# Series of products that nobody reads, taken out of TensorE's program at every seam between stages

## The chip, the cores and the metric

One core of one Trainium2 chip. The metric is device time in microseconds (us); the kernel before took 1933.99 us, the median of 3 runs from 1933.72 to 1934.06.

## What is computed

Two models run one after the other on 256 tokens of width 1024, in float32, each with two layers.

- **First block** (twice): `h = rmsnorm(x) @ w_in`; three groups of attention heads on slices of h; `x += heads @ w_o`; then a feed-forward, `x += (silu(g) * u) @ w_down` with `g, u` the halves of a short causal convolution over `rmsnorm(x) @ w_up` (2 x 2816 columns). One more rmsnorm ends it.
- **Second block** (twice): a mixer (retention and HGRN2 heads on `rmsnorm(h) @ w_in`, 4608 columns, then `@ w_out`), and a mixture of 16 experts. `softmax(xn @ w_router)` gives each expert its 32 best tokens (top-k), and `ye = (silu(xe @ w_gate) * (xe @ w_up)) @ w_down`, times the gate, is added back to the tokens. A last rmsnorm gives the output.

## The kernel before

Every engine has one program, written out by hand; semaphores order them. The residual X stays in SBUF as two tiles of 128 tokens. Weights stream in through one hardware queue that SP issues, into a ring (6 slots in the first block, 12 and an arena beside them in the second); SP waits on `slot_free[s]`, which TensorE counts up behind the last product that reads a slot.

Between two stages stands a norm. ScalarE takes sums of squares (line 717, into XN), VectorE adds them (728), GpSimd takes the power -1/2 (736), VectorE and ScalarE scale one tile of 128 tokens each into XN (732 and 724). `turn_normed` (740) waits for these and transposes XN, four transposes to each of four PSUM banks (all at line 749); VectorE and ScalarE copy the banks to XT, and the next stage's products read XT: lines 2346 to 2348 (`up` of the feed-forward), 2099 to 2101 (first block's input), 2066 (the mixer's first block of columns). In the first block and in the mixer weights and activations are each split in two rounded parts, and every product is three.

Routing (2546 to 2558): logits (2520), softmax on VectorE and ScalarE, two transposes of the affinities (2549), four rounds of top-8 on VectorE (1971, 1973), two transposes of the slots (2554), one-hot rows (1987), and then, for each of four groups of four experts, `gather` (2579), products with quarters of the array (2621, 2639) for gate, up and down, and `scatter` (2671). In group 0 each block of weights is a separate piece (2621); later ones come in pairs (2639), and the very last block (the last `single_quad` of group 3) comes in two halves, waited for one after the other. `turn_gates` (2564) transposes the gates.

TensorE's queue is in order, so what stands in its program is carried out there. `idle_products(bank, n)` (2056) is n products of the identity with itself, 128x128, into a PSUM bank whose content nobody reads before it is written again. It stands at these places, with no wait ahead of it:

| where | n | line | times |
|---|---|---|---|
| before `turn_normed` of the feed-forward | 12 | 2332 | 2 |
| before `turn_normed` of the first block's second layer | 20 | 2072 | 1 |
| before `turn_normed` of the first mixer | 40 | 2388 | 1 |
| before `turn_normed` of the second mixer | 12 | 2388 | 1 |
| before the wait for the softmax | 5 | 2546 | 2 |
| before the wait for the top tokens | 20 | 2551 | 2 |
| before the wait for the one-hot rows | 6 | 2557 | 2 |
| before the last block of the last group | 7 | 2657 | 2 |

```python
def idle_products(bank, n):

    for _ in range(n):
        nc.tensor.matmul(psum[:, bank, 0:P], ident, ident, start=True, stop=True)
...
idle_products(4, IDLE_PRODUCTS["feed-forward"])
turn_normed(pe, past, 2, 1)
```

Of the kernel before, what the change touches and what calls it, by code (L numbers as in the profile page):

```python
# [15 lines left out]
P = 128  # L16
# [58 lines left out]
N_GROUPS = EXPERTS // GROUP  # L75
# [7 lines left out]
PAIRS = D // 256  # L83
# [19 lines left out]
ITEM_AT = {item: n for n, item in enumerate(ITEMS)}  # L103
EXP_LN_SET = "natural_log_exp_and_others"

IDLE_PRODUCTS = {"first block": 20, "feed-forward": 12, "first mixer": 40, "expert sums": 12,
                 "softmax": 5, "top tokens": 20, "one-hot rows": 6, "last quad": 7}
C2_N1, C2_N2, C2_LB, C2_OML, C2_FLAG, NPAR2 = 0, 8, 16, 20, 24, 28


# [32 lines left out]
def four_rows(k):  # L143

    return slice(4 * P * (k // 4) + k % 4, 4 * P * (k // 4 + 1), 4)
# [166 lines left out]
def build(nc, w, out):  # L312
    ctx = ExitStack()
    with ctx:
# [3 lines left out]
        def sem(name):  # L318
            return ctx.enter_context(nc.semaphore(name))
# [6 lines left out]
        psum = ctx.enter_context(nc.psum_tensor("psum", [P, 8, 512], F32))  # L326
# [22 lines left out]
        def place(n):  # L349
            at = cursor[0]  # L350
            cursor[0] += n
            assert cursor[0] <= ARENA, cursor[0]
            return arena[:, at:at + n]
# [9 lines left out]
        one = place(1)  # L363
# [5 lines left out]
        def const(name, rows=P):  # L369
            at, n = where1[name]  # L370
            return cst[0:rows, at:at + n]

        ident = const("ident")
# [11 lines left out]
        rows = place(DEPTH * 2 * P).rearrange("p (l t n) -> p l t n", l=DEPTH, t=2)  # L385
# [255 lines left out]
        top = sem("top_tokens_steps")  # L641
        slot_mm = sem("slots_turned")
        hot = sem("one_hot_rows")
# [19 lines left out]
        def before(p, g=0):  # L663

            blocks, groups = (min(p, DEPTH), max(p - DEPTH, 0)), N_GROUPS * max(p - DEPTH, 0) + g

            def past(sem):
                first, second, group = PER_PASS[sem.name]
                return first * blocks[0] + second * blocks[1] + group * groups

            return past
# [66 lines left out]
        def turn_normed(pe, past, n, nth):  # L738

            for b in range(4):  # L740
                if b % 2 == 0:
                    pe.wait_ge(xn_ready, past(xn_ready) + 2 * nth + b // 2 + 1)
                    pe.wait_ge(xn_act, past(xn_act) + 2 * nth + b // 2 + 1)
                turn_bank(b).then_inc(turned, 1)
# [126 lines left out]
        block = ctx.enter_context(nc.Block())  # L871
# [1158 lines left out]
        def _(pe):  # L2030
# [10 lines left out]
            def release(over, value, slots):  # L2041

                if pending:
                    last_over, last_value, last_slots = pending.pop()
                    pe.wait_ge(last_over, last_value)
                    for s in last_slots:
                        pe.sem_inc(slot_free[s], 1)
                if slots:
                    pending.append((over, value, slots))
# [3 lines left out]
                pe.sem_clear(slot_loaded[s])  # L2053
                return slot(s)

            def idle_products(bank, n):

                for _ in range(n):
                    nc.tensor.matmul(psum[:, bank, 0:P], ident, ident, start=True, stop=True)

            def columns_product(out, wt, c0, m, fresh=None):

                for k in range(KD):
                    if fresh is not None:
                        wait_turned(pe, past, fresh, k)
                    last = nc.tensor.matmul(out, wt[:, k, c0:c0 + m], XT[:, k, :], start=(k == 0), stop=(k == KD - 1))
                return last

            for lay in range(DEPTH):
                past = before(lay)  # L2070
                if lay:
                    idle_products(7, IDLE_PRODUCTS["first block"])
                turn_normed(pe, past, 0, 0)

                def use(i):
# [61 lines left out]
                for k in range(2):  # L2137
                    for t in range(TT):
                        last = nc.tensor.transpose(psum[:, 0, (2 * k + t) * P:(2 * k + t + 1) * P],
                                                   cqn[:, t, k * P:(k + 1) * P], ident)  # L2140
                last.then_inc(latT, 1)
                for t in range(TT):
                    last = nc.tensor.transpose(psum[:, 1, t * P:(t + 1) * P], ckvn[:, t, :], ident)
# [5 lines left out]
                for b in range(2):  # L2149
                    for h in range(2):  # L2150
                        for k in range(2):
                            c = (2 * b + h) * MLA_QK
                            last = nc.tensor.matmul(psum[0:MLA_QK, 2 + b, h * S:(h + 1) * S], wuq[:, k, c:c + MLA_QK],
                                                    cqT[:, k, :], start=(k == 0), stop=(k == 1))
                    last.then_inc(mla_mm, 1)

                for b in range(2):
                    for h in range(2):
                        c = (2 * b + h) * (NOPE + MLA_V)
                        last = nc.tensor.matmul(psum[0:NOPE, 4 + b, h * S:(h + 1) * S], wukv[:, c:c + NOPE], ckvT,  # L2160
                                                start=True, stop=True)
                    last.then_inc(mla_mm, 1)
                wv = wukv.rearrange("p (h n) -> p h n", h=MLA_H)[:, :, NOPE:NOPE + MLA_V]
                for t in range(TT):
                    last = nc.tensor.matmul(psum[:, 0, t * S:(t + 1) * S], ckvT[:, t * P:(t + 1) * P], wv,
                                            start=True, stop=True)
# [5 lines left out]
                                 start=True, stop=True).then_inc(mla_mm, 1)  # L2172
# [3 lines left out]
                for b in range(2):  # L2176
                    pe.wait_ge(mla_q, past(mla_q) + b + 1)
                    for h in range(2):
                        last = nc.tensor.matmul(psum[0:MLA_QK, 2 + b, h * S:(h + 1) * S], const("turn", MLA_QK),
                                                mqr[0:MLA_QK, 2 * b + h, :], start=True, stop=True)  # L2180
# [148 lines left out]
                    project_last_heads(i).then_inc(wo_mm, 1)  # L2329
                    release(wo_mm, past(wo_mm) + i + 1, [(SPLIT_IN + i) % SLOTS_1])  # L2330
                release(None, 0, [])
                idle_products(4, IDLE_PRODUCTS["feed-forward"])
                turn_normed(pe, past, 2, 1)
                release(None, 0, [])

# [49 lines left out]

            for lay in range(DEPTH):
                past = before(DEPTH + lay)
                idle_products(7, IDLE_PRODUCTS["expert sums" if lay else "first mixer"])
                turn_normed(pe, past, 0, 0)

                def split_product(out, token_major, m, w1, w2):
# [84 lines left out]
                for t in range(TT):  # L2476
                    for h in range(HEADS):
                        for i in range(TT):
                            last = nc.tensor.matmul(psum[:, t, h * HD:(h + 1) * HD], ST[:, i, t, h, :],
                                                    hi[:, i, h * HD:(h + 1) * HD], start=(i == 0), stop=(i == 1))  # L2480
                    last.then_inc(h_mixed, 1)
                pe.wait_ge(emp_dve, past(emp_dve) + 8)
                for t in range(TT):
                    for h in range(HEADS):
                        for i in range(TT):
                            last = nc.tensor.matmul(psum[:, 2 + t, h * HD:(h + 1) * HD], RS[:, h, i, t * P:(t + 1) * P],
                                                    rv[:, i, h * HD:(h + 1) * HD], start=(i == 0), stop=(i == 1))
# [55 lines left out]
                turn_raw(3)  # L2543
                raw_logits(2)
                raw_logits(3).then_inc(logits, 1)
                idle_products(3, IDLE_PRODUCTS["softmax"])
                pe.wait_ge(soft, past(soft) + 3)
                for t in range(TT):
                    last = nc.tensor.transpose(psum[0:EXPERTS, 5, t * P:(t + 1) * P], aff[:, t, :], ident)
                last.then_inc(affT_mm, 1)  # L2550
                idle_products(3, IDLE_PRODUCTS["top tokens"])
                pe.wait_ge(top, past(top) + 2 * (CAP // 8) + 3)
                for t in range(TT):
                    last = nc.tensor.transpose(psum[:, 4, t * EXPERTS:(t + 1) * EXPERTS], slotT[:, t * P:(t + 1) * P],
                                               ident[0:EXPERTS, 0:EXPERTS])
                last.then_inc(slot_mm, 1)
                idle_products(3, IDLE_PRODUCTS["one-hot rows"])

                def turn_gates():
                    pe.wait_ge(gated_hot, past(gated_hot) + TT)  # L2560
# [9 lines left out]
                for g in range(N_GROUPS):  # L2570
# [5 lines left out]
                    def gather(b):  # L2576
                        for k in (2 * b, 2 * b + 1):
                            for t in range(TT):
                                last = nc.tensor.matmul(psum[:, 4 + b, (k % 2) * P:(k % 2 + 1) * P], XN[:, t, four_rows(k)],
                                                        one_hot[:, t, g, :], start=(t == 0), stop=(t == 1))  # L2580
                        last.then_inc(xe_mm, 1)
# [69 lines left out]
                    def product(mat, src, bank, done):  # L2651
                        for half in range(2):
                            if (g, mat, half) in SINGLE:
                                for pair in (2 * half, 2 * half + 1):
                                    single_quad(mat, pair, src, bank, done)
                                    if (g, pair) == (N_GROUPS - 1, PAIRS - 2):
                                        idle_products(4, IDLE_PRODUCTS["last quad"])
                                    if mat == 0 and pair < PAIRS - 1:
                                        gather(pair + 1)
                            else:  # L2660
                                if mat == 0 and half == 0:
                                    gather(2)
                                    gather(3)
                                if mat == 0:
                                    pe.wait_ge(xe_ready, past(xe_ready) + 2 * half + 2)
                                double_quad(mat, half, src, bank, done)
# [18 lines left out]
                    for c in range(2):  # L2685
                        pe.wait_ge(g_hid, past(g_hid) + c + 1)
                        for i in range(4):
                            last = nc.tensor.transpose(psum[:, 4 + c, i * P:(i + 1) * P], hid[:, c, four_rows(i)], ident)  # L2688
# [34 lines left out]
```

## Time and profile before

| | |
|---|---|
| median of 3 runs | 1933.99 us |
| the profiled execution's own time | 1935.1 us |
| its span | 1933.3 us |
| mean granted clock of TensorE | 0.907 |
| PE busy, share of the span | 1552.9 us, 80% |
| PEld (weight loads) | 1174.7 us, 61% |
| DVE / ACT / POOL | 735.9 / 568.3 / 61.5 us |
| DMA, mean | 290 GB/s |

The stages in order of time: first block, layer 0 to 344 us and layer 1 to 677 us; first mixer to 858 us; routing and experts to 1302 us; second mixer to 1479 us; routing and experts to the end. PEclk is the clock that the throttle granted to TensorE, 1.00 for 2.4 GHz and 0.50 for 1.2 GHz. A matmul's end is modelled, so the distance between starts says more than one duration. One product of line 2059 (float32) is two records of MATMUL; a transpose is one. In a timeline, what stands in brackets is the engine's idle time before the row and what ended it.

### The profile page before, as it was taken

The numbers are of one execution on the slowest core, as the hardware profiler recorded it, in microseconds if no ns is written. First come the engines' busy times: TensorE is split into PE (matmuls) and PEld (weight loads), VectorE is DVE, ScalarE is ACT, GpSimd is POOL, SyncE is SP. The second block draws the span as 40 slices with busy tenths as digits, with TensorE's granted clock in tenths as the row PEclk, the third lists the DMA queues.
The fourth block names the chain that finished last, engine by engine and source line by source line (L and its number), as shares of the span: only waits on it lengthen the run. The fifth ranks groups of instructions, "written<-read, shape, count | busy, mean of one in ns | idle before, by whom it ended". The sixth has DMA issues, their size and how long they took to land.

```text
span 1933.3 us, 26259 instructions
## 1 busy us (share of the span) xinstructions
PE 1552.9 (80%) x11300; PEld 1174.7 (61%) x11300; DVE 735.9 (38%) x1156; ACT 568.3 (29%) x914; POOL 61.5 (3%) x57
## 2 busy tenths in 40 slices
PE   7999999999999999997654747479999773565646
PEld 7899999999999899983211313139998230121212
DVE  4556666556666678630100101008963010010101
ACT  3455445445545476320000000018521000000001
POOL 0010000101000000000000000002010000000000
PEclk9999999999999999999777878789999886787878
DMA  9317555431755284589999999998458999999997
GB/s 290 120 41 239 177 194 185 127 110 58 244 177 193 88 261 149 177 352 372 427 428 427 427 428 427 427 401 273 134 196 333 419 427 427 427 427 428 428 426 309
DMA packets 174169, 560.84 MB, mean 290 GB/s; under 512 B 12200, under 2 KB 134486, under 8 KB 146278
## 3 DMA queue, kind: packets, MB, share of 16 engines
q1 hardware_dynamic: 165558, 551.49, 73.5%
q10 hardware_dynamic: 8496, 7.67, 1.3%
q8 instruction: 90, 1.47, 0.3%
q14 instruction: 25, 0.20, 0.0%
HBM read 558.09 MB, written 1.05 MB: 289 GB/s over the span
## 4 chain that ended last, share of the span: by engine, by line
PE 48%; issue 22%; DMA 17%; PEld 7%; DVE 2%; ACT 1%; SPq 1%; POOL 0%; POOLq 0%; PEldq 0%; ACTq 0%; another core or an unknown queue 0%; DVEq 0%
PE psum L2398 10%; PE psum L2639 5%; DMA ring<-in_w_down 3%; DMA ring<-in_w_gate 3%; DMA ring<-in_w_up 3%; PE psum L2502 3%; PE psum L2370 3%; DMA ring<-in_w_in 3%; PE psum L2346 2%; PE psum L2348 2%; PE psum L2347 2%; PEld psum L2370 2%; PE psum L2621 2%; PE psum L2272 2%; PEld psum L2348 2%
## 5 line engine op out<-in xcount | busy, mean ns | idle before, releaser
L2639 PE MATMUL psum<-ring,arena 128*32 128x512 f32 (+1 forms) x1600 | 282.9, 696 | 181.0 <-DMA ring<-in_w_down 74.2
L2639 PE MATMUL psum<-arena 128*32 128x512 f32 x1024 | 209.4, 706 | 142.2 <-DMA arena<-in_w_down 39.9
L868 DVE TENSOR_TENSOR W<-ring,W 128x2048 fp32r<-128x2048 f32 (+1 forms) x96 | 214.0, 2229 | 167.4 <-ACT W L863 167.0
L2639 PEld LDWEIGHTS psum<-ring,arena 128*32 128x32 f32 x1600 | 70.4, 128 | 330.2 <-issue 327.1
L863 ACT ACTIVATE W<-ring 128x2048 fp32r<-128x2048 f32 (+1 forms) x96 | 178.6, 1861 | 110.4 <-PE psum L2348 68.3
L2346 PE MATMUL psum<-XT,W 128*128 128x256 f32 x704 | 199.9, 284 | 0.1
L2639 PEld LDWEIGHTS psum<-arena 128*32 128x32 f32 x1024 | 50.4, 127 | 244.8 <-issue 244.6
L2347 PE MATMUL psum<-XT,W 128*128 128x256 f32 x704 | 199.1, 283 | 0.0
L2348 PE MATMUL psum<-XT,W 128*128 128x256 f32 x704 | 199.1, 283 | 0.0
L2398 PE MATMUL psum<-rounded_slot,rounded_slot 128*128 128x256 f32 x1312 | 188.0, 284 | 0.8 <-DVE rounded_slot L1810 0.8
L2004 DVE TENSOR_TENSOR arena<-arena,psum 128x512 f32<-128x512 f32 x16 | 11.0, 690 | 434.0 <-PE psum L2639 434.0
L2398 PEld LDWEIGHTS psum<-rounded_slot,rounded_slot 128*128 128x128 f32 x1312 | 170.3, 192 | 1.9 <-DVE rounded_slot L1810 1.6
L2346 PEld LDWEIGHTS psum<-XT,W 128*128 128x128 f32 x704 | 133.9, 190 | 1.3 <-DVE XT L832 0.5
L2347 PEld LDWEIGHTS psum<-XT,W 128*128 128x128 f32 x704 | 133.9, 190 | 0.8
L2348 PEld LDWEIGHTS psum<-XT,W 128*128 128x128 f32 x704 | 133.9, 190 | 0.0
L2370 PE MATMUL psum<-W,hT 128*128 128x512 f32 x504 | 119.3, 392 | 0.8 <-DVE hT L1723 0.8
L2370 PEld LDWEIGHTS psum<-W,hT 128*128 128x128 f32 x504 | 93.1, 188 | 20.7 <-DVE hT L1723 1.7
L2007 DVE COPY arena<-psum 128x512 f32<-128x512 f32 x6 | 4.2, 693 | 234.1 <-PE psum L2639 234.1
L1446 ACT ACTIVATE arena<-psum 128x512 f32<-128x512 f32 x16 | 9.6, 599 | 262.7 <-PE psum L2688 261.7
L1450 ACT ACTIVATE arena<-psum 128x512 f32<-128x512 f32 (+1 forms) x12 | 6.3, 528 | 263.5 <-PE psum L2639 204.3
L1441 ACT ACTIVATE arena<-psum 128x512 f32<-128x512 f32 x16 | 9.4, 599 | 252.3 <-PE psum L2639 252.3
L1709 DVE SCALAR_TENSOR_TENSOR arena<-psum,arena 128x255 f32<-128x255 f32 (+1 forms) x176 | 72.6, 475 | 5.0 <-ACT arena L1252 4.2
(302 smaller groups left out, 2554.1 us busy)
## 6 DMA issues: line engine op xcount, KB each, us to landing
ring<-in_w_down SPq DMA_DIRECT2D x36, 2048.0 KB, 29.4
ring<-in_w_up SPq DMA_DIRECT2D x32, 2048.0 KB, 28.9
ring<-in_w_up SPq DMA_DIRECT2D x58, 1024.0 KB, 5.2
ring<-in_w_in SPq DMA_DIRECT2D x56, 1024.0 KB, 5.9
ring<-in_w_gate SPq DMA_DIRECT2D x28, 2048.0 KB, 33.2
arena<-in_w_up SPq DMA_DIRECT2D x24, 2048.0 KB, 32.3
arena<-in_w_down SPq DMA_DIRECT2D x20, 2048.0 KB, 29.4
arena<-in_w_gate SPq DMA_DIRECT2D x20, 2048.0 KB, 30.0
```

What stands on the lines that cost most here:

```text
L863: nc.scalar.activation(W1[split_pair(v)][:, c], slot(s)[:, c], ACT.Copy).then_inc(rounded, 1)
L868: nc.vector.tensor_tensor(W2[split_pair(v)][:, c], slot(v % SLOTS_1)[:, c], W1[split_pair(v)][:, c].bitcast(F32), ALU.subtract).then_inc(r ...
L1709: last = nc.vector.scalar_tensor_tensor(out=dst, in0=psum[:, 4 + 2 * (j % 2) + g, m * S:m * S + S - tap], scalar=par[:, col + c:col + c + ...
L2272: last = nc.tensor.matmul(dst, a[:, k, rows], b[:, k, :], start=(t == n == 0 and k == 2), stop=False, skip_group_check=True)
L2346: nc.tensor.matmul(dst, w1[:, k, c], XT1[:, k, :], start=(k == 0), stop=False)
L2347: nc.tensor.matmul(dst, w1[:, k, c], XT2[:, k, :], start=False, stop=False)
L2348: last = nc.tensor.matmul(dst, w2[:, k, c], XT1[:, k, :], start=False, stop=(k == KD - 1))
L2370: last = nc.tensor.matmul(psum[:, 2 * t + c, :], a, b[:, m, 512 * c:512 * (c + 1)], start=(j == 0 and m == 0 and b is w1 and a is h1), sto ...
L2398: last = nc.tensor.matmul(out, a, b, start=(k == n == 0), stop=(k == KD - 1 and n == 2))
L2502: last = nc.tensor.matmul(psum[:, 4 + i, t * S:(t + 1) * S], XT[:, k, t * P:(t + 1) * P], wt[:, k, :], start=(t == 0 and k == 4), stop=(k ...
L2621: last = nc.tensor.matmul(psum[CAP * e:CAP * (e + 1), b, 0:cols.stop - cols.start], src[:, 2 * pair + k, CAP * e:CAP * (e + 1)], tiles[e][ ...
L2639: last = nc.tensor.matmul(psum[CAP * e:CAP * (e + 1), b, 0:cols.stop - cols.start], src[:, 4 * half + k, CAP * e:CAP * (e + 1)], tiles[e][ ...
```

## The change

All eight calls go, with the function and the table of counts. Nothing is added, and no wait is moved.

```diff
-IDLE_PRODUCTS = {"first block": 20, "feed-forward": 12, "first mixer": 40, "expert sums": 12,
-                 "softmax": 5, "top tokens": 20, "one-hot rows": 6, "last quad": 7}
...
-            def idle_products(bank, n):
-
-                for _ in range(n):
-                    nc.tensor.matmul(psum[:, bank, 0:P], ident, ident, start=True, stop=True)
...
-                if lay:
-                    idle_products(7, IDLE_PRODUCTS["first block"])
                 turn_normed(pe, past, 0, 0)
...
-                idle_products(4, IDLE_PRODUCTS["feed-forward"])
                 turn_normed(pe, past, 2, 1)
...
-                idle_products(7, IDLE_PRODUCTS["expert sums" if lay else "first mixer"])
                 turn_normed(pe, past, 0, 0)
...
-                idle_products(3, IDLE_PRODUCTS["softmax"])
                 pe.wait_ge(soft, past(soft) + 3)
...
-                idle_products(3, IDLE_PRODUCTS["top tokens"])
                 pe.wait_ge(top, past(top) + 2 * (CAP // 8) + 3)
...
-                idle_products(3, IDLE_PRODUCTS["one-hot rows"])
...
                                     single_quad(mat, pair, src, bank, done)
-                                    if (g, pair) == (N_GROUPS - 1, PAIRS - 2):
-                                        idle_products(4, IDLE_PRODUCTS["last quad"])
```

## Rows read from the trace of the kernel before

**Rows 1.** Windows, all engines: columns are window and length, busy time (instructions), PEclk, DMA, GB/s.
```profile
200.00:300.00 100.00, 100.00 (x713) 94.41 (x712) 66.64 (x78) 50.48 (x52) 0.00 (x0) 1.00 0.56 184
800.00:900.00 100.00, 93.47 (x646) 75.95 (x648) 28.82 (x68) 17.03 (x57) 9.86 (x7) 1.00 0.82 322
```

**Rows 2.** Groups of instructions by line, engine PE: the series that goes.
```profile
L2059 PE MATMUL psum<-arena 128*128 128x128 f32 x344 | 41.3, 277 | 1.2 <-PE psum L2361 0.9
```

**Rows 3.** Timeline of PE at the kernel's start: start, duration, engine, line, tiles, wait.
```profile
10.73 3.65 PE L749 MATMUL psum<-arena,XN 128*128 128x128 f32 x16 [1.47 <-ACT XN L724]
16.28 0.55 PE L2099 MATMUL psum<-W,XT 128*128 128x256 f32 x1 [1.90 <-issue]
...
21.54 0.41 PE L2099 MATMUL psum<-W,XT 128*128 128x256 f32 x1
...
22.16 0.28 PE L2099 MATMUL psum<-W,XT 128*128 128x256 f32 x1
...
22.52 0.28 PE L2099 MATMUL psum<-W,XT 128*128 128x256 f32 x1
```

**Rows 4.** Windows in the expert stage, columns as in rows 1.
```profile
923.00:924.00 1.00, 0.01 (x2) 0.02 (x2) 0.00 (x0) 0.00 (x0) 0.00 (x0) 0.50 1.00 426
926.00:927.00 1.00, 1.00 (x8) 0.18 (x4) 0.00 (x0) 0.00 (x0) 0.00 (x0) 0.67 1.00 426
932.00:933.00 1.00, 0.36 (x4) 0.00 (x0) 0.00 (x0) 0.00 (x0) 0.00 (x0) 1.00 0.96 410
936.00:937.00 1.00, 0.00 (x0) 0.00 (x0) 0.00 (x0) 0.00 (x0) 0.00 (x0) 0.95 1.04 442
```

**Rows 5.** Waits of PE; then a window, second layer, columns as in rows 1.
```profile
PE psum L2564 <- POOL arena L1087: 4.5, 2, 2.3
...
1516.00:1518.00 2.00, 1.03 (x6) 1.03 (x7) 0.00 (x0) 0.02 (x1) 0.92 (x1) 0.79 0.99 401
```

**Rows 6.** Timeline of PE before the first feed-forward.
```profile
143.60 7.07 PE L2281 MATMUL psum<-ring,XT 128*128 128x256 f32 x32
...
154.28 1.96 PE L749 MATMUL psum<-arena,XN 128*128 128x128 f32 x16 [0.55 <-ACT XN L724]
```

**Rows 7.** Timeline before the second layer of the first block.
```profile
344.44 4.63 PE L2059 MATMUL psum<-arena 128*128 128x128 f32 x40
...
347.73 1.33 ACT L724 ACTIVATE XN<-X,arena 128x512 f32<-128x512 f32 x2 [1.59 <-POOL arena L736]
...
348.90 1.93 PE L749 MATMUL psum<-arena,XN 128*128 128x128 f32 x16
```

**Rows 8.** Timeline before the first mixer.
```profile
677.74 9.17 PE L2059 MATMUL psum<-arena 128*128 128x128 f32 x80 [0.91 <-PE psum L2361]
...
684.13 1.34 ACT L724 ACTIVATE XN<-X,arena 128x512 f32<-128x512 f32 x2 [1.13 <-POOL arena L736]
...
686.75 1.94 PE L749 MATMUL psum<-arena,XN 128*128 128x128 f32 x16
```

**Rows 9.** Timeline of PE before the second mixer.
```profile
1302.12 2.00 PE L2671 MATMUL psum<-arena 128*128 128x256 f32 x8
...
1307.45 1.96 PE L749 MATMUL psum<-arena,XN 128*128 128x128 f32 x16 [0.66 <-DVE XN L732]
```

**Rows 10.** Chain that ended last, first routing, in order of time; then one timeline row.
```profile
857.74 1.86 PE psum L2520 x16
...
867.45 1.53 PE psum L2059 x12
868.98 1.88 PE psum L2579 x8
...
871.44 3.64 PE psum L2621 x32
...
867.71 1.44 DVE L1987 TENSOR_TENSOR arena<-arena 128x128 f32<-128x128 f32 x4
```

**Rows 11.** Timeline of PE at the end of the last group.
```profile
1921.51 1.94 PE L2621 MATMUL psum<-arena 128*32 128x256 f32 x32 [0.55 <-DMA arena<-in_w_down]
```

## The prediction

> **What bounds the kernel now.** I read the windows first, then the chain of waits, then the timeline at each place where the change cuts. The windows show two regimes. In the feed-forward TensorE is busy all of the time and the DMA engines little over half of it, at 0.56 [rows 1]; the same holds in the rest of the first block and in the mixers, so a microsecond that TensorE loses there is lost at the end. In the expert stages the DMA engines are full and TensorE waits for weights, at a clock that falls and returns all the time [rows 4]; there TensorE has time to give. The border matters: in 800 to 900 us DMA is at 0.82, not yet full, and the chain through the routing and into the first group of experts runs through TensorE and VectorE, not through a transfer [rows 1, 10]. What TensorE loses in the routing therefore still moves the DMA stream behind it.
>
> The line that goes has 344 records, 172 products, 41.3 us of busy time [rows 2]. Little of it is on the path: the series stand where TensorE would wait for a norm or for the top tokens. So the first question is what time they cost, the second what the clock does without them.
>
> **What two clocks mean in time.** At the start three split products take 0.62 to 0.64 us (the start at 21.54 to that at 22.16) and right behind it 0.36 us (22.16 to 22.52) [rows 3]: that is 1.2 against 2.4 GHz, although the granted clock's column reads 1.00 there. Of a cold microsecond of dense products 0.44 us is lost (1 - 0.36 / 0.64). The sixteen transposes of a turn take 3.65 us cold [rows 3] and 1.96 warm [rows 6]: 1.7 us lost.
>
> When does it fall? After the last product at 932.4 it fell at 936.9, 4.5 us later (a mean of 0.95 over the microsecond is nine tenths of it at 1.00 and one at 0.50) [rows 4]. Behind the first group's gate products TensorE waits 2.3 us for GpSimd in both layers [rows 5], then does a microsecond of transposes: in the second layer the clock fell at 1517.2, 2.5 us after the last product; in the first it stayed at 1.00 through 900 us [rows 1]. So with a pause of 2.3 us and transposes behind it the clock is lost one time in two, and nothing here shows it kept over more than 4.5 us. When does it return? After 924.0 at 926.7 (2.7 us) [rows 4]; at the start, where dense products begin at 16.28, at 22.1 (5.8 us) [rows 3]. The middle is 4.25 us, worth 1.9 us of loss; the ends are 1.2 and 2.55.
>
> **The change part by part.** Each series is taken with what stands in its place.
>
> - *Feed-forward, twice.* The last product before it ends at 150.67, the turn starts at 154.28 behind its own wait of 0.55 us for ScalarE's XN [rows 6], so taking the 24 records away gains nothing. TensorE is then without a product for 3.6 us, and for 5.6 us until the first dense one, with transposes in between. That is more than the 2.3 and 3.4 us that lost the clock in one of two cases [rows 5]; I take it as lost, before or within the turn: 1.0 of its 1.7 us, and 1.9 behind it, less 0.1 for what VectorE is ahead with. 2.8 us each, 5.6 in all. Ends: 0, if the clock is kept; 4.25, if it falls before the turn and returns late.
> - *Second layer of the first block.* XN's first half is ready half-way through the row of ScalarE, at 348.4, and the turn starts at 348.90 without a wait, behind the last of 40 records [rows 7]: 0.3 us to gain, with the 0.2 us from a release to a start. The pause is 4.2 us (344.4 to 348.6), 6.1 to the dense products. Loss 1.3 + 1.9, net 2.9 us. Ends: -0.3 and 3.95.
> - *First mixer.* The longest series, 80 records. ScalarE's first half ends at 684.8, the turn could start at 685.0 and starts at 686.75 [rows 8]: 1.75 us gained, the one real gain of the change. But TensorE has then done nothing since 676.8, for 8.2 us, and the clock is surely down: the turn takes 1.7 us longer, which gives the gain back exactly, and the dense part adds 1.9. Net 1.85 us. Ends: -1.75 (clock kept, which only a kernel unlike this one would show) and 2.5.
> - *Second mixer.* The pause is 3.35 us (1304.1 to 1307.45), and 5.2 to the dense products; the turn waits for XN as it is [rows 9], no gain. 0.9 + 1.9 = 2.8, rounded to 2.7 since this is the shortest of the pauses. Ends: 0 and 4.25.
> - *Routing, twice, three series.* TensorE's real work stops at 859.6 and the gathers start at 868.98, behind the last 12 records [rows 10]. What gathers wait for, the second one-hot of four, is ready half-way through VectorE's row, at 868.43 [rows 10]: 0.5 us gained. In the 8.9 us between stand four small transposes; the clock falls. These are on VectorE's chain and take 0.1 us more each by the turn's rows (1.7 / 16): 0.4 at most, 0.3 taken. Then come gathers of 1.88 us and products of 3.64 us [rows 10]. No row has a cold gather. From below it costs nothing more, from above it doubles; it runs at 0.235 us a record where the turn's take 0.12, so something other than the array paces it, and I take a third of the doubling, 0.6. The rest of a cold 4.25 us falls on the quarter-array products, 1.7 us at 0.44: 0.75. Net 0.6 + 0.75 + 0.3 - 0.5 = 1.15 each, 2.3 in all. Ends: -0.1 and 2.5 each. What is late next is the release of slots behind the first gates, and DMA starts later by as much.
> - *Last block, twice.* The products behind it run 128x256 for their second half and wait 0.55 us for the weights at 1921.51 [rows 11]: the transfer sets the end, and TensorE is only ahead of it. TensorE's pause without the series is under 2 us, between stretches of full work. Nothing, both times; if that cover failed, the end has 1.94 us of such products and would take 0.44 / 0.56 of it more, 1.5 us.
>
> Sum: 5.6 + 2.9 + 1.85 + 2.7 + 2.3 = 15.35 us. From the profiled execution's own 1935.1 us to 1950.4; the median of the runs lies 1.1 below that execution, so **1949.3 us**, 0.8% slower. The ends of all terms together are -2.3 and 24.9, which no run will meet at once: where the clock returns differs from seam to seam.
>
> **A rule beside the rows.** The turn of 3.65 us at the start did not lift the clock, and 5.8 us of products behind it did [rows 3]. The Trainium skill (TensorE: Matmul & The Clock Gate, Part 4: PE-mode transpose) says that a transpose does not count as work for the clock; by it the short pauses are the longer ones of each pair above and all lost, the sum of 15.35 us, and without it the first rival's 7.
>
> **The rivals.**
>
> 1. *The turn counts as work, and the short pauses are mostly survived.* Then only the first mixer and the two routings are surely cold, and cold for less: their turn already lifts the clock. For it: 2.3 us of wait and a microsecond of transposes kept the clock in one of two layers [rows 5]. Against it: the start [rows 3]. The four short pauses would lose in some six of ten cases 1.7 us each, 4.1; less 0.3 gained; the first mixer 0.2; the routings 2.3 or a little more: 6.3 to 7.5, **1941 us**.
> 2. *Not slower.* The clock holds wherever a pause is under 9 us, or is back by the first dense product, and the earlier starts are all that is left: 1.75 + 0.3 + 2 x 0.5 = 3.05 us, **1931 us**. It decides at the first mixer: if the turn at 685.0 runs in 1.96 us, this is it. Against it, the fall 4.5 us after 932.4 [rows 4]. That the change does nothing at all (the series absent from the machine's program, say) is excluded by their records [rows 2].
> 3. *More than the terms.* A gather that doubles, returns as late as at the start of the kernel, and a second fall in a seam with many small waits: 1.3 us more per routing and 0.65 at each of the five turns, 6, **1955 us** and above.
>
> **How the numbers follow.** The forecast (clock lost at all seven seams, returns in the middle) has 0.60, with its own range 1945 to 1955; the first rival 0.26; the second 0.07; the third 0.07. A measurement of this kernel can tell 0.2%, 3.9 us, from no change. Faster by more than that needs more than every gain I found: 0.02. Within: the rest of the second rival and the low end of the first, 0.08. Slower: 0.90. The range from 1939 to 1956 leaves out the second rival and the outer part of the third, under 0.2 in all. I expect the runs of the changed kernel to differ by more than the 0.3 us of before, since the place of a return need not repeat.
>
> **What would show it.** In the changed kernel's windows the granted clock should read below 1.00 near 155, 349, 487, 685, 864, 1308 and 1485 us, each shifted by what was lost before it. The turn behind the first mixer's norm should start 1.7 us earlier against its XN and take over 3 us. In the expert stages nothing but an offset. I am wrong if the turns still take 1.96 us, if a seam is later by the norm and not by TensorE, or if the offset after 870 us is not carried to the end.

## The result and the profile after

The changed kernel takes 1941.04 us (median of 5 runs, 1940.73 to 1944.82) against 1933.94 (5 runs, 1933.42 to 1934.06): a ratio of 1.0041, 95% interval 1.0028 to 1.0054. It is 7.1 us slower. The profiled execution is the longest of the five, 1944.82 us with a span of 1943.0. In a later job the same kernel took 1943.57 against 1934.16 (1.0044, interval 1.0030 to 1.0057).

From the page of the changed kernel, the busy time of TensorE and the granted clock by slices:

```profile
PE 1523.6 (78%) x10956; PEld 1144.5 (59%) x10956; DVE 736.2 (38%) x1156; ACT 568.5 (29%) x914; POOL 61.5 (3%) x57
...
PEclk9999999999999999999777868779998987686868
```

29.3 us of busy time are gone with 344 records, and the mean clock went from 0.907 to 0.893. Slices of 48 us are too coarse to show where; the seams have to be read one by one.

**A ledger.** GpSimd's instructions are the same in both kernels and lie between the seams, so the difference of the start times of one of them is what was lost or gained up to there. Two of them, before (timeline of POOL):

```profile
152.69 0.70 POOL L736 TENSOR_TENSOR arena<-arena 128x2 f32<-128x2 f32 x1 [35.88 <-DVE arena L728]
...
347.00 0.69 POOL L736 TENSOR_TENSOR arena<-arena 128x2 f32<-128x2 f32 x1 [193.62 <-DVE arena L728]
```

and after:

```profile
151.68 0.69 POOL L734 TENSOR_TENSOR arena<-arena 128x2 f32<-128x2 f32 x1 [35.88 <-DVE arena L726]
...
347.04 0.70 POOL L734 TENSOR_TENSOR arena<-arena 128x2 f32<-128x2 f32 x1 [194.66 <-DVE arena L726]
```

The first is 1.01 us early, the second 0.04 us late: the feed-forward's seam between them cost 1.05 us. The same subtraction for all seams, for the profile of the change and for a second profile of the same kernel (e10_changed_again below):

| seam | between GpSimd's starts before | forecast | first profile | second profile |
|---|---|---|---|---|
| start of the kernel | to 35.69 | 0 | -0.99 | -1.01 |
| feed-forward, layer 0 | 152.69, 347.00 | 2.8 | +1.05 | +0.99 |
| first block, layer 1 | 347.00, 367.96 | 2.9 | +1.95 | +1.90 |
| feed-forward, layer 1 | 484.95, 678.72 | 2.8 | +2.23 | +2.21 |
| first mixer | 683.34, 800.21 | 1.85 | -0.17 | -0.20 |
| routing, layer 0 | 858.62, 894.21 | 1.15 | +2.21 | +2.18 |
| experts, layer 0 | 894.21, 1305.80 | 0 | +0.28 | +0.05 |
| second mixer | 1305.80, 1323.89 | 2.7 | +1.49 | +1.63 |
| routing, layer 1 | 1479.27, 1514.87 | 1.15 | +2.18 | +2.46 |
| experts, layer 1, to the end | 1514.87, 1926.98 | 0 | -0.54 | +0.57 |

The rest (35.69 to 152.69, 367.96 to 484.95, 678.72 to 683.34, 800.21 to 858.62, 1323.89 to 1479.27) moves by 0.02 us at most: where TensorE is busy, what is lost stays lost. The change costs 6.55 us at the five norms and 4.4 in the two routings of the profiled execution. With the other rows (-0.99, +0.28, -0.54) that is 9.7 us, the difference of the two spans; the medians differ by 7.1, and which seams cost less in the runs between cannot be read, since only the longest was profiled. The -0.99 us of the first row has nothing to do with the change (see the start, below).

**The turns.** Timeline of PE in the changed kernel, each turn (line 747) and the first product behind it; they answer to [rows 6 to 9]:

```profile
153.28 3.55 PE L747 MATMUL psum<-arena,XN 128*128 128x128 f32 x16 [3.61 <-ACT XN L722]
156.58 0.38 PE L2336 MATMUL psum<-XT,W 128*128 128x256 f32 x1
...
348.63 3.65 PE L747 MATMUL psum<-arena,XN 128*128 128x128 f32 x16 [4.00 <-ACT XN L722]
351.93 0.56 PE L2090 MATMUL psum<-W,XT 128*128 128x256 f32 x1
...
689.23 3.53 PE L747 MATMUL psum<-arena,XN 128*128 128x128 f32 x16 [8.16 <-DVE XN L730]
692.59 7.07 PE L2059 MATMUL psum<-XT,ring 128*128 128x256 f32 x32
...
1314.01 3.46 PE L747 MATMUL psum<-arena,XN 128*128 128x128 f32 x16 [3.34 <-DVE XN L730]
1317.30 7.07 PE L2059 MATMUL psum<-XT,ring 128*128 128x256 f32 x32
```

The turns take 3.46 to 3.65 us instead of 1.96: they run at 1.2 GHz. From a turn's start to the first product behind it pass 3.3 to 3.4 us, where the kernel before needs 1.8 to 2.0. The pauses ahead of the turns, in brackets, are 3.6, 4.0, 8.2 and 3.3 us. The fifth turn, before the second feed-forward, starts at 488.54 behind a pause of 3.61 us, takes 3.65 us, and has its first product at 491.83. Now the granted clock (windows; the last three figures are PEclk, DMA, GB/s):

```profile
156.00:157.00 1.00, 1.00 (x8) 1.00 (x7) 0.93 (x4) 0.99 (x4) 0.00 (x0) 0.70 1.10 348
354.00:355.00 1.00, 1.00 (x8) 1.00 (x8) 0.07 (x1) 0.00 (x0) 0.00 (x0) 0.71 1.19 166
494.00:495.00 1.00, 1.00 (x8) 1.00 (x8) 0.11 (x1) 0.85 (x1) 0.00 (x0) 0.74 1.11 358
692.00:693.00 1.00, 1.00 (x7) 0.97 (x6) 0.94 (x2) 0.25 (x2) 0.00 (x0) 0.75 1.11 351
1317.00:1318.00 1.00, 1.00 (x8) 0.92 (x7) 0.53 (x1) 0.50 (x2) 0.00 (x0) 0.93 1.10 347
880.00:881.00 1.00, 1.00 (x12) 0.12 (x4) 0.00 (x0) 0.00 (x0) 0.00 (x0) 0.88 0.00 0
```

A mean of 0.70 over the microsecond from 156 is a return at 156.6; of 0.75 from 692, one at 692.5; of 0.93 from 1317, one at 1317.1. Up to these three returns TensorE had done nothing but transposes since its pause: the first products behind the turns start at 156.58, 692.59 and 1317.30, the first of them within 0.03 us of the return. In the first block's second layer the clock came back at 354.6 and in the second feed-forward at 494.5, each 2.7 us behind the first product.

**The routing**, which answers to [rows 10]:

```profile
865.44 0.39 PE L2537 MATMUL psum<-arena 128*16 128x128 f32 x2 [1.78 <-DVE arena L1963]
871.22 0.39 PE L2541 MATMUL psum<-arena 16*128 16x16 f32 x2 [5.39 <-DVE arena L1979]
872.42 2.24 PE L2565 MATMUL psum<-arena,XN 128*128 128x128 f32 x8 [0.81 <-DVE arena L1985]
875.25 6.09 PE L2607 MATMUL psum<-ring,arena 128*32 128x512 f32 x32 [0.59 <-DVE arena L1995]
881.27 2.13 PE L2565 MATMUL psum<-arena,XN 128*128 128x128 f32 x8
```

The clock fell at 866.6 and returned at 880.2 (0.88 in the window from 880 above), 7.8 us behind the first gather. The small transposes in between lost 0.1 us: VectorE starts the one-hot rows at 871.87, which is 867.71 [rows 10] plus the 4.06 us of the ledger, and 0.1 more. The eight records of the gather take 2.24 us instead of 2.03 in the same view; the 32 quarter products take 6.0 us to the next start (875.25 to 881.27) instead of 3.6 [rows 10]. That is the whole loss: 2.4 + 0.2, less 0.46 us gained since the gather starts when the one-hot rows are ready.

### The profile page after: what moved, and what is told of

It reads as the page before. It is cut to its first block, busy times and chain, and to the rows that moved or that the text cites. A ratio compares the mean times of both kernels' runs of the same rounds, so it can differ in the third digit from the quotient of the medians.

```text
span 1943.0 us, 25571 instructions
## 1 busy us (share of the span) xinstructions
PE 1523.6 (78%) x10956; PEld 1144.5 (59%) x10956; DVE 736.2 (38%) x1156; ACT 568.5 (29%) x914; POOL 61.5 (3%) x57
## 3 DMA queue, kind: packets, MB, share of 16 engines
HBM read 558.09 MB, written 1.05 MB: 288 GB/s over the span
## 4 chain that ended last, share of the span: by engine, by line
PE 47%; issue 22%; DMA 18%; PEld 7%; DVE 3%; ACT 2%; SPq 1%; POOL 0%; ACTq 0%; POOLq 0%; PEldq 0%; another core or an unknown queue 0%; DVEq 0%
PE psum L2387 10%; PE psum L2625 5%; DMA ring<-in_w_down 3%; DMA ring<-in_w_up 3%; DMA ring<-in_w_gate 3%; PE psum L2491 3%; DMA ring<-in_w_in 3%; PE psum L2360 3%; PE psum L2336 2%; PE psum L2337 2%; PE psum L2338 2%; DMA arena<-in_w_up 2%; PEld psum L2360 2%; PE psum L2263 2%; PEld psum L2338 2%
```

## The experiments

Each is the kernel before with the edit shown. All of one job ran on one chip beside the kernel before (medians 1934.13, 1934.49 and 1934.16 us in the three jobs; its runs lie between 1931.1 and 1936.6). A seam's amount in a profile is read off the ledger as above.

### Are transposes work for the clock?

```diff
-                for _ in range(n):
-                    nc.tensor.matmul(psum[:, bank, 0:P], ident, ident, start=True, stop=True)
+                for _ in range(2 * n):
+                    nc.tensor.transpose(psum[:, bank, 0:P], ident, ident)
```

> All eight series stay, but each product (two records) is two transposes of the identity instead. Theory A (the loss is TensorE's clock, and transposes are work for the clock as products are; in the changed kernel the clock returned at 156.6 us, before the first product behind the turn): the clock stays at 1.00 through all seams and the time is that of the kernel before, 1934 within 1.5 us. Theory B (my forecast's: transposes are no work for the clock): the clock falls at every seam as in the changed kernel, and the time is 1941 us or more, since the earlier starts of the changed kernel are missing as well.

Measured: 1933.75 us, ratio 0.9997 (0.9989 to 1.0006). Timeline of PE at the first mixer and two windows:

```profile
677.95 8.95 PE L2059 MATMUL psum<-arena 128*128 128x128 f32 x80 [0.94 <-PE psum L2361]
686.75 1.94 PE L749 MATMUL psum<-arena,XN 128*128 128x128 f32 x16
...
684.00:685.00 1.00, 1.00 (x12) 1.00 (x11) 0.74 (x2) 0.68 (x2) 0.23 (x1) 1.00 1.22 315
862.00:866.00 4.00, 4.00 (x38) 3.90 (x36) 3.69 (x14) 1.35 (x3) 0.00 (x0) 1.00 1.02 426
```

The series has its 80 records and the turn behind it takes 1.94 us; the clock reads 1.00 in the middle of the longest series and in that of the top tokens. No seam moved by over 0.2 us up to 1479 us. Theory A stands: transposes hold the clock as well as products do. The Trainium skill (TensorE: Matmul & The Clock Gate, Part 4: PE-mode transpose) says that a transpose does not count as work for the clock; for these float32 transposes the measurement decides.

The second routing moved by +0.51 us in this profile. There the clock fell at 1480.0 (0.58 in the mean from 1480 to 1484), while TensorE went from the logits to the softmax's series without a gap, so that series began cold. In e3_norms_dropped and e7_mixer_dropped below, which leave all three series of the routing in place, the clock fell there too and the second routing moved by +0.50 and +0.20. So a series in place does not always keep the clock, and an amount at the second routing is good to 0.5 us only.

### Which seams cost

```diff
# e2_routing_dropped
-                 "softmax": 5, "top tokens": 20, "one-hot rows": 6, "last quad": 7}
+                 "softmax": 0, "top tokens": 0, "one-hot rows": 0, "last quad": 7}
# e3_norms_dropped
-IDLE_PRODUCTS = {"first block": 20, "feed-forward": 12, "first mixer": 40, "expert sums": 12,
+IDLE_PRODUCTS = {"first block": 0, "feed-forward": 0, "first mixer": 0, "expert sums": 0,
# e5_last_dropped
-                 "softmax": 5, "top tokens": 20, "one-hot rows": 6, "last quad": 7}
+                 "softmax": 5, "top tokens": 20, "one-hot rows": 6, "last quad": 0}
# e7_mixer_dropped
-IDLE_PRODUCTS = {"first block": 20, "feed-forward": 12, "first mixer": 40, "expert sums": 12,
+IDLE_PRODUCTS = {"first block": 20, "feed-forward": 12, "first mixer": 0, "expert sums": 12,
```

> Only the three series of the routing are left out (softmax, top tokens, one-hot rows), in both layers; the norms' series and the last block's stay. By the ledger of the changed kernel's profiled run each routing cost 2.2 us at the first gates' end: 4.4 us in sum, so 1938.3 us, with a spread under 1 us since both fall for sure. Theory of my forecast: 1.15 us each, 1936.2 us. If the DMA stream hid it, 1934.

Measured: 1936.59 us, 1.0011 (1.0003 to 1.0020), 2.5 us more: my forecast's 1936.2, and not the ledger's 1938.3. The profile has +1.60 in the first routing and +1.04 in the second, less than the changed kernel's 2.2: the clock returned at 873.7 there, 6.2 us behind the first gather. What decides when the clock returns there, and so why the median is this low, is not settled.

> Only the series before the five turns are left out (feed-forward twice, first block, both mixers). If the parts add up to the changed kernel's median (7.1 us) and the routing has 4.4: 2.7 us, 1936.6 us, and runs that differ by 2 us or more, because it is here that the clock's fall depends on the run. By the ledger of the one profiled run (1.05 + 1.95 + 2.2 - 0.2 + 1.5): 6.5 us, 1940.4 us. My forecast's terms: 13 us, 1947 us.

Measured: 1940.35 us (6 runs, 1937.79 to 1942.98), 1.0030 (1.0018 to 1.0042), 6.2 us more: the ledger's 6.5, not the 2.7 that the first median left over, and not my 13. Its profile has +1.0, +1.95, +2.25, -0.2 and +2.25 at the five norms, 7.3 in sum, and 2.6 us less at the start of the kernel, so the nearness of 6.2 to 6.5 is in part luck. The second mixer cost 2.25 us instead of the 1.5 of the changed kernel, since the clock came back at 1315.5 there, 2.5 us behind the first product (1313.06), and not before it:

```profile
1315.00:1316.00 1.00, 1.00 (x4) 0.82 (x4) 0.03 (x1) 1.00 (x2) 0.00 (x0) 0.74 1.10 349
```

The two parts sum to 8.7 us; the whole had 7.1 in one job and 9.4 in the other.

> Only the series of 7 products before the last block of the last group is left out, in both layers. Its cover is the transfer of the last weights: no change, 1934.1 within 0.6 us. If the pause of under 2 us brought the clock down at the end: 1.5 us more, 1935.6.

Measured: 1933.89 us, 0.9999 (0.9990 to 1.0008). The last block in its profile:

```profile
1916.49 1.93 PE L2621 MATMUL psum<-arena 128*32 128x512 f32 x16 [1.74 <-DMA arena<-in_w_down]
...
1921.82 1.94 PE L2621 MATMUL psum<-arena 128*32 128x256 f32 x32 [0.58 <-DMA arena<-in_w_down]
```

TensorE now waits 1.74 us for the first halves and, as before, half a microsecond for the last ones, so the transfer ends the stage with the series or without.

> Only the series of 40 before the first mixer is left out. The clock falls for sure in 8.2 us, the turn starts 1.75 us sooner against its XN and takes 1.7 us longer, and the turn itself has lifted the clock by the first dense products, as in the changed kernel's profile: 0 within 0.5 us, 1934.1. My forecast's term, with the return counted from the dense products: plus 1.85, 1936.0.

Measured: 1933.91 us, 0.9998 (0.9989 to 1.0007). Timeline and window:

```profile
683.94 3.30 PE L749 MATMUL psum<-arena,XN 128*128 128x128 f32 x16 [8.17 <-DVE XN L732]
687.08 7.07 PE L2066 MATMUL psum<-XT,ring 128*128 128x256 f32 x32
...
686.00:687.00 1.00, 1.00 (x8) 1.00 (x7) 0.23 (x1) 0.75 (x2) 0.00 (x0) 0.62 1.11 349
```

8.17 us of pause, a turn of 3.30 us that started 1.7 us sooner against the norm, and the clock back at 686.8, before the first product at 687.08. The seam is worth -0.40 us in this profile. The longest of the series buys nothing at its length.

### Half the length, and one series alone

```diff
# e6_half
-IDLE_PRODUCTS = {"first block": 20, "feed-forward": 12, "first mixer": 40, "expert sums": 12,
-                 "softmax": 5, "top tokens": 20, "one-hot rows": 6, "last quad": 7}
+IDLE_PRODUCTS = {"first block": 10, "feed-forward": 6, "first mixer": 20, "expert sums": 6,
+                 "softmax": 2, "top tokens": 10, "one-hot rows": 3, "last quad": 3}
# e11_top_dropped
-                 "softmax": 5, "top tokens": 20, "one-hot rows": 6, "last quad": 7}
+                 "softmax": 5, "top tokens": 0, "one-hot rows": 6, "last quad": 7}
```

> Every series has half its products (10, 6, 20, 6, 2, 10, 3, 3). Theory A says that a pause costs only if the clock falls in it. The first mixer's turn starts at once when XN is ready (1.75 us gained), first block 0.3, one-hot rows 0.45 twice; the pauses that come back are 2.2 us before the feed-forwards, 2.1 and 3.0 before the first block's second layer and the first mixer, 1.9 before the second mixer, 3.1 within the routing, none much above the 2.3 us that lost the clock one time in two. If two in three of them keep it: 1934 within 1.5 us. If a pause costs in proportion to its length (the rival: a slow restart after waiting, no matter the clock): half of the change's loss, 1937.5.

Measured: 1937.07 us, 1.0012 (1.0004 to 1.0021), with runs from 1933.55 to 1940.50, the widest of all. My 1934 within 1.5 us was missed, and by the median the rival looks right; the profile (1939.24 us) says that it is not. Four seams cost nothing or gain: 0.0 at both feed-forwards, -0.3 in the first block, -1.73 at the first mixer, with pauses of 1.9, 1.9, 1.8 and 2.5 us ahead of their turns. The loss is in three: +2.4 in each routing and +1.65 at the second mixer. One row of each kind:

```profile
868.87 5.92 PE L2621 MATMUL psum<-ring,arena 128*32 128x512 f32 x32 [0.59 <-DVE arena L1997]
...
1307.01 3.60 PE L749 MATMUL psum<-arena,XN 128*128 128x128 f32 x16 [2.00 <-DVE XN L732]
```

The quarter products from 868.87 take 5.92 us and the turn 3.60, behind pauses of 3.16 and 2.00 us: cold. So a pause costs nothing where the clock holds, and 1.65 to 2.4 us here where it falls. Its length alone does not say which: 2.5 us held it and 2.00 lost it, in one and the same execution. That the wide spread of the runs comes from this is likely, but only one run was profiled.

> Only the series of 20 before the wait for the top tokens is left out, twice; those for the softmax and the one-hot rows stay. A pause of 5.4 us in the middle of the routing, 1.5 us of products, then the gathers. If the gathers are too thin to lift the clock (in the changed kernel it returned 7.8 us behind the first of them, and 5 us behind the first quarter product): it falls and comes back late, 1.0 to 2.7 us per routing, 1936.1 to 1939.5. If 6 products and the gathers lift it in time: under 1 us, 1935.

Measured: 1937.24 us, 1.0016 (1.0008 to 1.0025), 3.1 us more; +1.31 and +1.30 in the profile's routings. The amount is that of the late return, the reason is another:

```profile
866.15 2.93 PE L2059 MATMUL psum<-arena 128*128 128x128 f32 x12
868.87 1.95 PE L2579 MATMUL psum<-arena,XN 128*128 128x128 f32 x8
871.41 3.64 PE L2621 MATMUL psum<-ring,arena 128*32 128x512 f32 x32 [0.59 <-DVE arena L1997]
```

The clock had fallen in the pause of 5.4 us (at 862.9), and the six products of the one-hot rows, cold, took 2.7 us to the gather's start instead of 1.4. They lifted it (back at 869.7), and the quarter products at 871.41 ran at their 3.64. A series that begins cold makes itself late: the lost time moved from the work into the filler.

### The better kernel, and the start

```diff
# e4_trimmed
-IDLE_PRODUCTS = {"first block": 20, "feed-forward": 12, "first mixer": 40, "expert sums": 12,
-                 "softmax": 5, "top tokens": 20, "one-hot rows": 6, "last quad": 7}
+IDLE_PRODUCTS = {"first block": 18, "feed-forward": 12, "first mixer": 32, "expert sums": 12,
+                 "softmax": 5, "top tokens": 20, "one-hot rows": 4, "last quad": 7}
```

> Three series are shortened so that they end when what TensorE waits for is ready, and nothing else changes: first mixer 40 to 32 products, first block 20 to 18, one-hot rows 6 to 4. If the clock is all that the series are for, it stays up and the earlier starts are gained: 1.75 + 0.3 + 2 x 0.45, near 3.0 us, 1931.0 us. If a pause right behind a series already brings the clock down, or XN is not what the turn waits for: 1934 or more.

Measured: 1931.23 us, 0.9984 (0.9975 to 0.9992), 2.9 us less than the kernel before. The ledger has -0.28, -1.73, -0.44 in the first three places and -0.19 in the second routing. The first mixer:

```profile
674.81 7.38 PE L2059 MATMUL psum<-arena 128*128 128x128 f32 x64 [0.91 <-PE psum L2361]
682.07 1.96 PE L749 MATMUL psum<-arena,XN 128*128 128x128 f32 x16
```

64 records, and the turn behind them at full clock, 1.7 us sooner.

What is left is the start. In every profile up to here the first turn is wholly or mostly cold (3.28 to 3.65 us). The first dense products run cold until 20 to 22.5 us in some, as in [rows 3]. In others they are warm from the first one on (e3_norms_dropped, e4_trimmed), and in two they begin warm and the clock reads 0.50 from 18 to 20 us (e2_routing_dropped, e7_mixer_dropped). Warm, in e4_trimmed, they start 0.11 to 0.12 us apart instead of 0.21:

```profile
16.36 0.28 PE L2100 MATMUL psum<-W,XT 128*128 128x256 f32 x1
16.47 0.28 PE L2101 MATMUL psum<-W,XT 128*128 128x256 f32 x1
```

The start moves GpSimd's instruction at 35.69 by 0.3 to -2.7 us from profile to profile, although none of the edits up to here touches it (the -0.99 of the ledger is this): 0 to +0.3 us where the dense products are cold until 22 us, -0.7 to -1.3 where they are cold until 20 or warm only in part, -2.6 and -2.7 where they are warm throughout. The edit, on top of e4_trimmed, with 20 and 13 products in e8_start and 11 and 7 in e9_start_short:

```diff
             pe.wait_ge(s_small, SMALL)
+            for _ in range(11):
+                nc.tensor.matmul(psum[:, 3, 0:P], ident, ident, start=True, stop=True)
             pe.wait_ge(s_rows, ROWS)
...
                 pe.wait_ge(s_par, 2 * DEPTH)
+                if not lay:
+                    idle_products(7, 7)
```

> The trimmed counts of before, and two series more where the kernel before has none: 20 products as soon as the identity is loaded, ahead of the first turn, and 13 between the first turn and the first split product of the first block. Theory A: the start, which in each profile so far ran cold until 19 to 22 us, runs at 1.00, as in those profiles that were 2.7 us early at 36 us; against the trimmed kernel 1.3 us in the median, 1929.8, and a narrower spread. If the start hangs on the transfers or on ScalarE's splits: 1931.2, the trimmed kernel's time.

Measured: 1932.22 us, 0.9988 (0.9979 to 0.9997), not the 1929.8 expected: 2.3 us under the kernel before, where the trimmed kernel was 2.9 under it in its own job. The two intervals overlap, so the long series gained nothing that can be told. Ten of the eleven runs lie within 2.5 us, where the trimmed kernel's eleven lie within 3.2 (the eleventh took 3771 us, and nothing explains it; the ratio leaves it out). The start:

```profile
6.10 6.51 PE L2035 MATMUL psum<-arena 128*128 128x128 f32 x40 [6.10 <-DMA arena<-first_constants]
...
12.89 1.93 PE L749 MATMUL psum<-arena,XN 128*128 128x128 f32 x16
```

40 records begun cold take 6.5 us, and the turn, itself warm, starts at 12.89, 2.2 us later than in [rows 3]. GpSimd's instruction is 1.1 us early.

> The trimmed counts, and the two series at the start at half the length: 11 products ahead of the first turn and 7 behind it, so that neither makes the turn or the first split product late (with 20 and 13 the turn started at 12.89 instead of 10.9). If the clock at the start is what is left to gain: 1929.7, and runs within 1 us of each other, as with the long series. If 11 cold products do not lift it: the trimmed kernel's 1931.2 and its spread.

Measured: 1930.18 us, 0.9981 (0.9972 to 0.9989), all eleven runs within 2.3 us, not within the 1 us expected. This is the lowest median: 4.0 us under the kernel before and 13.4 under the changed one, beside both on the same chip. Its lead over the trimmed kernel (0.9981 against 0.9984, in different jobs) is not clear of noise.

```profile
6.00 5.07 PE L2035 MATMUL psum<-arena 128*128 128x128 f32 x22 [6.00 <-DMA arena<-first_constants]
...
11.45 1.92 PE L749 MATMUL psum<-arena,XN 128*128 128x128 f32 x16
```

The turn still starts 0.7 us late (11.45 against 10.73 [rows 3]) but runs in 1.92 us. GpSimd's instruction is 2.5 us early, as much as in the trimmed kernel's profile (2.7), which had no series there. That the two series make such a start the rule and not the exception is the likely gain, but no run shows it by itself.

### The changed kernel once more

> The changed kernel itself, unchanged, once more, for a second profile and for its time beside the runs of the kernel before of this chip. By the ledger (1.05 + 1.95 + 2.2 - 0.2 + 2.2 + 1.5 + 2.2) less what falls well in other runs: 7 to 9 us over the kernel before. The seams' amounts should differ from those of the first profile wherever the clock falls or returns at another moment, by up to 2 us at a seam, and be the same elsewhere.

Measured: 1943.57 us, 1.0044 (1.0030 to 1.0057). The amount was a little above the 7 to 9 expected (9.4); that the seams would differ did not come true. The table above has both profiles, and they agree within 0.3 us up to the last expert stage. They are not two independent samples: up to the second mixer every fall and every return of the clock in the second profile lies within 0.2 us of the first's (156.4 and 156.6, 692.3 and 692.5, 880.0 and 880.2, 1316.9 and 1317.1). Where the clock returns at another moment the same seam costs another amount, as the second mixer did in e3_norms_dropped. Both profiles are also the longest of their five runs. The medians (7.1 and 9.4 us) differ by no more than the noise: the intervals of the two ratios cover each other almost wholly.

## Why the prediction was right, and where it was not

The direction and the mechanism were right, the size was not: 7.1 us measured against 15.35 forecast.

- *The bound, and that losses are carried.* Right. Between the seams nothing moves by more than 0.02 us, and the routing's 2.2 us pass into the expert stage as a later stream and stay to the end.
- *The clock falls at all seven seams.* Right: at 153.2, 347.8, 487.7, 685.7, 866.6, 1313.7 and 1491.2 us of the first profile, and the second lost as much at each. Rival 1's pauses that are survived did not occur there; they did in e6_half, with pauses of 1.8 to 2.5 us.
- *The return, counted from the first dense product, 1.9 us behind each turn.* This is the step that failed. In it the turn was no work for the clock. Three of the five returns came by the end of the turn, and e1_transposes shows why: transposes are work. The other two came 2.7 us behind the first product, 1.2 us of loss by the prediction's own 0.44. So the five terms of 1.9 us, 9.5 in all, were 2.4. The turns themselves were priced a little low: 1.3 to 1.6 us more to the first product, five times, where the sum had 1.0, 1.0, 1.3, 1.7 and 0.9. Seam by seam: feed-forward 1.05 and 2.2 instead of 2.8, first block 1.95 instead of 2.9, second mixer 1.5 instead of 2.7, and the first mixer -0.2 instead of 1.85, since there the gain of 1.75 us stood against the cold turn alone. Sum of the five: 13.05 forecast, 6.55 found in the profile, 6.2 in e3_norms_dropped's median.
- *The routing, 1.15 each.* Right in the median of e2_routing_dropped (1.2 each), too small in the profiles: 2.2 to 2.5 in both of the changed kernel, 1.6 and 1.0 in that of e2_routing_dropped. Its terms were wrong in either case, and in part against each other. The gather, of which I doubled a third (0.6), costs 0.2 more when cold; the small transposes cost 0.1 instead of 0.3. The return was counted 4.25 us behind the first gather and came 7.8 behind it (6.2 in e2_routing_dropped), so that the cold stretch takes in nearly all of the first 32 quarter products (2.4 us), where I had put 0.75. That the gather lifts the clock badly would explain it, but no run isolates that.
- *The last block, nothing.* Right (e5_last_dropped: 0.9999).
- *No gain but 3.05 us of earlier starts.* Right, and e4_trimmed collects them: 2.9 us in the median, 2.6 at the seams of its profile.
- *The runs differ more than before.* True of the first job (4.1 us against 0.6). In the later jobs the kernel before spans 2.9 to 5.5 us itself, so it says little.
- *Forecast and range.* 1949.3 was 8.2 us too high, and 1941.04 lies outside the 1945 to 1955 that the forecast gave itself. The range as a whole holds it near its low end, at the first rival's 1941. (The upper ends of all terms add up to 24.2 and not to 24.9; nothing hangs on it.) That rival had the right mechanism at the turns (the turn counts as work) and the right sum by two errors: it let short pauses survive, and it kept my price of the routing. That it hit the number is luck.

## What to carry to other kernels

Work that nobody reads can be worth its place. TensorE's clock fell at each of the seven seams from which the series were taken, so price a seam by what the clock does behind it, and not by whether an instruction is on the path. Fit such a series to the wait it fills, neither longer (it delays the turn by itself, 1.75 us here) nor begun after the clock is down (it is then cold itself), and leave it out where a transfer ends the stage anyway. A ledger of the start times of one mostly idle engine in two traces splits a total of 0.4% into its seams. Within a trace it reads to 0.02 us where TensorE is busy; what a seam costs still differs between executions, by 0.75 us at the second mixer here.

## What was not expected of the hardware

- Float32 transposes of 128x128 hold and lift TensorE's clock: series made of them gave 1933.75 against 1934.13 us, and in the changed kernel the clock returned by the end of three turns, with nothing but transposes since the pause.
- The gather's products (128x128, 0.235 us a record warm) are almost indifferent to the clock, 2.24 against 2.03 us for eight. Behind them it came back late, 7.8 us after the first of them; whether they are the reason is open.
- Two profiles of one kernel had the same seams' amounts within 0.3 us up to the last expert stage, and up to the second mixer the clock's falls and returns at the same moments within 0.2 us, although its five runs spread over 4 to 5 us.
- With the series in place the clock still fell in three profiles at the second routing (e1_transposes, e3_norms_dropped, e7_mixer_dropped), and that seam cost 0.2 to 0.5 us more; in e1_transposes it fell at 1480.0 with no gap in TensorE's rows before it.
